# Retention chunk products from one unrounded pass to three rounded passes, in a hybrid decoder kernel on one core

## What is computed

```python
scores = jnp.einsum('bnihd,bnjhd->bnhij', q, k) * intra
inner = jnp.einsum('bnhij,bnjhe->bnihe', scores, v)
k_dec = k * jnp.exp((C - 1 - idx)[:, None] * log_g[None, :])[:, :, None]
kv = jnp.einsum('bnjhd,bnjhe->nbhde', k_dec, v)
...
state * chunk_decay + kv_n, state
...
q_dec = q * jnp.exp((idx + 1.0)[:, None] * log_g[None, :])[:, :, None]
cross = jnp.einsum('bnihd,nbhde->bnihe', q_dec, state_start)
return (inner + cross).reshape(B, S, H, DV)
```

## Time and profile before

| | us |
|---|---|
| median of three runs | 2712.46 |
| the profiled execution | 2713.61 |
| its span on the core | 2711.8 |
| PE busy | 2661.3 |
| VectorE busy | 1643.1 |
| GpSimd busy | 862.8 |
| ScalarE busy | 625.8 |

### The profile page before, as it was taken

One profiled execution on the slowest core, in us unless ns is written; L12 is line 12 of the kernel. 1 busy time (PEld: TensorE's weight loads), 2 busy tenths in 40 slices (PEclk: granted clock), 3 DMA queues, 4 the chain that ended last, 5 costly groups with the idle time before them and its releaser, 6 DMA issues.

```text
span 2711.8 us, 39266 instructions
## 1 busy us (share of the span) xinstructions
PE 2661.3 (98%) x14674; PEld 2260.8 (83%) x14674; DVE 1643.1 (61%) x3712; ACT 625.8 (23%) x1259; POOL 862.8 (32%) x467
## 2 busy tenths in 40 slices
PE   7999999999999999999999999999999999999998
PEld 5888888888888888788878888888888888888886
DVE  6778777877754433534578778777877434453333
ACT  5333333333311111200142332333332111120001
POOL 3333333333321212434542333333332122243443
PEclk9999999999999999999999999999999999999999
DMA  4322222122211112323532222222222111133244
GB/s 169 95 75 63 76 71 82 57 83 64 83 41 39 43 36 71 121 93 118 160 95 83 75 74 65 71 75 78 61 81 62 42 49 41 40 103 100 94 140 140
DMA packets 292832, 217.79 MB, mean 80 GB/s; under 512 B 31682, under 2 KB 246036, under 8 KB 292388
## 3 DMA queue, kind: packets, MB, share of 16 engines
q1 hardware_dynamic: 254322, 151.21, 19.1%
q10 hardware_dynamic: 38322, 64.07, 6.8%
HBM read 176.37 MB, written 38.86 MB: 79 GB/s over the span
## 4 chain that ended last, share of the span: by engine, by line
PE 82%; DVE 7%; DMA 3%; POOL 3%; issue 2%; SPq 1%; ACT 1%; ACTq 0%; DVEq 0%; POOLq 0%
PE dense_ps L739 20%; PE dense_ps L743 20%; PE dense_ps L741 20%; PE work L722 3%; PE dense_ps L763 2%; PE dense_ps L764 2%; PE dense_ps L765 2%; DMA arena<-l_scratch 1%; PE work L975 1%; POOL w_lo L2161 1%; PE work L1012 1%; PE work L951 1%; PE work L934 1%; PE work L1032 1%; PE work L1094 1%
## 5 line engine op out<-in xcount | busy, mean ns | idle before, releaser
L739 PE MATMUL dense_ps<-act_hi,w_hi 128*128 128x512 f32 x2560 | 1065.4, 416 | 11.5 <-POOL act_lo L2182 5.3
L743 PE MATMUL dense_ps<-act_hi,w_lo 128*128 128x512 f32 x2560 | 1003.7, 392 | 0.0
L741 PE MATMUL dense_ps<-act_lo,w_hi 128*128 128x512 f32 x2560 | 1001.5, 391 | 0.0
L2161 POOL TENSOR_TENSOR w_lo<-w_raw,w_hi 128x1024 fp32r<-128x1024 f32 x174 | 435.0, 2500 | 1094.0 <-ACT w_hi L1229 554.1
L743 PEld LDWEIGHTS dense_ps<-act_hi,w_lo 128*128 128x128 f32 x2560 | 481.4, 188 | 106.8
L739 PEld LDWEIGHTS dense_ps<-act_hi,w_hi 128*128 128x128 f32 x2560 | 483.5, 189 | 98.4 <-issue 6.1
L741 PEld LDWEIGHTS dense_ps<-act_lo,w_hi 128*128 128x128 f32 x2560 | 484.2, 189 | 81.2 <-issue 0.2
L1675 DVE SCALAR_TENSOR_TENSOR arena<-arena,cols 128x512 f32<-128x512 f32 x288 | 239.9, 833 | 4.9
L1540 DVE CAST w_hi<-w_raw 128x1024 fp32r<-128x1024 f32 x92 | 67.1, 729 | 173.0 <-PE dense_ps L765 112.7
L722 PE MATMUL work<-mk,arena 128*128 128x128 f32 x768 | 113.8, 278 | 11.4 <-issue 7.5
L1689 DVE SCALAR_TENSOR_TENSOR arena<-arena 128x512 f32<-128x512 f32 x96 | 115.0, 1198 | 15.8 <-ACT arena L1235 15.7
(11 more groups left out here) (216 smaller groups left out, 3792.8 us busy)
## 6 DMA issues: line engine op xcount, KB each, us to landing
w_raw<-in_w_in SPq DMA_DIRECT2D x138, 512.0 KB, 3.7
gate_scratch<-arena ACTq DMA_DIRECT2D x64, 256.0 KB, 2.5
arena<-gate_scratch ACTq DMA_DIRECT2D x64, 256.0 KB, 2.9
arena<-l_scratch SPq DMA_DIRECT2D x62, 256.0 KB
w_raw<-in_w_out SPq DMA_DIRECT2D x18, 512.0 KB, 4.1
o_scratch<-arena ACTq DMA_DIRECT2D x32, 256.0 KB, 2.0
arena<-o_scratch ACTq DMA_DIRECT2D x32, 256.0 KB, 3.3
w_raw<-in_w_up_dn SPq DMA_DIRECT2D x16, 512.0 KB, 4.2
```

The lines of the kernel that those rows point to most:

```text
L739: eng.matmul(dense_ps[:, to, :], w_hi[:, slot, k, :], hi[:, k, seg], start=(k == 0), stop=False)
L741: eng.matmul(dense_ps[:, to, :], w_hi[:, slot, k, :], lo[:, k, seg], start=False, stop=False)
L743: mm = eng.matmul(dense_ps[:, to, :], w_lo[:, slot, k, :], hi[:, k, seg], start=False, stop=(k == KT - 1))
L2161: eng.tensor_tensor(w_lo[:, slot, :, :], w_from[second][:, :, :], w_hi[:, slot, :, :].bitcast(F32), ALU.subtract)\
```

## The change

Each operand of the three chunk products is split in a high part (rounded to float32r, by ACT) and a low part (operand minus high part, by DVE for keys, scores and states, by POOL for values and queries; it takes the operand's place). A product is now three rounded matmuls of 256 columns (`three`). The semaphores rop_f (operand ready), rop_h (high part ready), rop_v and rop_p (low parts ready) count the operands in the written orders. PE waits before a half's first chunk for the low parts of queries, values and scores, and before each queries-times-state product for the state's low part. In the second half 4 filling pieces instead of 2 stand before the chunks and 6 instead of 8 after them. The splits of both z weight blocks no longer wait for the values' block. In the last head, two instead of four delta blocks are rounded by ACT before the first tanh of the second half, the others after the states. Some buffers are placed anew in the arena to make room. The scores' product and the transposes are unchanged.

```diff
--- before
+++ after
+def in_order(*steps):
+    return {step: i + 1 for i, step in enumerate(steps)}
+OPERANDS = in_order("q0", "k0", "s0", "q1", "k1", "s1")
+HIGHS = in_order("v0", "q0", "k0", "s0", "state1", "state2", "state3", "state4", "v1", "q1", "k1", "s1", "state5", "state6", "state7")
+LOWS_VECTOR = in_order("k0", "s0", "state1", "state2", "state3", "state4", "k1", "s1", "state5", "state6", "state7")
+LOWS_POOL = in_order("v0", "q0", "v1", "q1")
...
+        rqd, rqd_lo, rqd_hi = parts("rqd", rt_at, [P, CPH, P])
+        rsc, rsc_lo, rsc_hi = parts("rsc", swap_at, [P, CPH, P])
+        _, rvt_lo = low_parts("rvt_of", rvt_at, [P, NCH, RDV])
...
@@ -671,8 +705,7 @@
                         load_w(m + 4 + j, w_src(l, w_in, RZ0 + j * P + h * RDV))
                     eng.wait_ge(rst_ok.sem, rst_ok.after(t, 0))
-                    eng.wait_ge(rsc_ok.sem, rsc_ok.after(t, 0))
-                    eng.wait_ge(rqd_ok.sem, rqd_ok.after(t, 0))
+                    eng.wait_ge(rop_f.sem, rop_f.after(t, 0))
                     eng.dma_start(rcon, ret[bass.ds(h, 1), :, :].rearrange("h p n -> p (h n)")).then_inc(rc_in.sem, 16)
...
+                    def three(to, a, b, start, stop):
+                        eng.matmul(to, a[0], b[0], start=start, stop=False)
+                        eng.matmul(to, a[0], b[1], start=False, stop=False)
+                        return eng.matmul(to, a[1], b[0], start=False, stop=stop)
...
-                        fill(5 if hf == 0 else 2)
-                        eng.wait_ge(rkd_ok.sem, rkd_ok.after(t, hf + 1))
-                        eng.wait_ge(rv_ok.sem, rv_ok.after(t, 4))
-                        eng.wait_ge(rsc_ok.sem, rsc_ok.after(t, hf + 1))
-                        eng.wait_ge(rqd_ok.sem, rqd_ok.after(t, hf + 1))
+                        fill(5 if hf == 0 else 4)
+                        eng.wait_ge(rop_p.sem, rop_p.after(t, LOWS_POOL[f"q{hf}"]))
+                        eng.wait_ge(rop_p.sem, rop_p.after(t, LOWS_POOL[f"v{hf}"]))
+                        eng.wait_ge(rop_v.sem, rop_v.after(t, LOWS_VECTOR[f"s{hf}"]))
                         for c in range(CPH):
                             cc = CPH * hf + c
                             if cc < NCH - 1:
                                 if c >= 2:
                                     eng.wait_ge(rst_ok.sem, rst_ok.after(t, cc - 1))
-                                eng.matmul(wk[(0, 5)[c % 2]][:, 0:RDV], rkd[:, c, :], rvt[:, cc, :], start=True, stop=True)\
-                                   .then_inc(rkv_ps.sem, 1)
+                                three(wk[(0, 5)[c % 2]][:, 0:RDV], (rkd_hi[:, c, :], rkd_lo[:, c, :]),
+                                      (rvt_hi[:, cc, :], rvt_lo[:, cc, :]), True, True).then_inc(rkv_ps.sem, 1)
                             dst = wk[4 if c < 2 else 1][:, (c % 2) * RDV:(c % 2 + 1) * RDV]
-                            mm = eng.matmul(dst, rsc[:, c, :], rvt[:, cc, :], start=True, stop=(cc == 0))
+                            mm = three(dst, (rsc_hi[:, c, :], rsc_lo[:, c, :]), (rvt_hi[:, cc, :], rvt_lo[:, cc, :]),
+                                       True, cc == 0)
                             if cc:
-                                eng.wait_ge(rst_ok.sem, rst_ok.after(t, cc))
-                                mm = eng.matmul(dst, rqd[:, c, :], rstate[:, cc % 2, :], start=False, stop=True)
+                                eng.wait_ge(rop_v.sem, rop_v.after(t, LOWS_VECTOR[f"state{cc}"]))
+                                mm = three(dst, (rqd_hi[:, c, :], rqd_lo[:, c, :]),
+                                           (rstate_hi[:, cc % 2, :], rstate_lo[:, cc % 2, :]), False, True)
                             mm.then_inc(ro_ps.sem, 1)
-                            fill(1 if c < CPH - 1 else 8)
+                            fill(1 if c < CPH - 1 else 8 if hf == 0 else 6)
                         for _ in fills:
                             pass
...
+                    def z_tanh(hf, e):
+                        eng.wait_ge(dense_ok[e].sem, dense_ok[e].after(m + BLK_RET + 4 + hf, 1))
+                        eng.wait_ge(rsz_ok.sem, rsz_ok.after(t, 2 * hf + e - 1))
+                        eng.activation(rth[:, e, :], dense_ps[:, e, :], ACT.Tanh, scale=0.5).then_inc(rth_ok.sem, 1)
+                    def values_hi(hf):
+                        four = slice(CPH * hf, CPH * hf + CPH)
+                        eng.wait_ge(rv_ok.sem, rv_ok.after(t, 4))
+                        eng.wait_ge(ro_ps.sem, ro_ps.after(t, 0))
+                        eng.activation(rvt_hi[:, four, :], rvt[:, four, :], ACT.Copy).then_inc(rop_h.sem, 1)
+                    values_hi(0)
                     for hf in range(NHALF):
+                        eng.wait_ge(rop_f.sem, rop_f.after(t, OPERANDS[f"q{hf}"]))
+                        eng.activation(rqd_hi[:, :, :], rqd, ACT.Copy).then_inc(rop_h.sem, 1)
+                        eng.wait_ge(rop_f.sem, rop_f.after(t, OPERANDS[f"k{hf}"]))
+                        eng.activation(rkd_hi[:, :, :], rkd, ACT.Copy).then_inc(rop_h.sem, 1)
+                        eng.wait_ge(rop_f.sem, rop_f.after(t, OPERANDS[f"s{hf}"]))
+                        eng.activation(rsc_hi[:, :, :], rsc, ACT.Copy).then_inc(rop_h.sem, 1)
                         if last and hf == 1:
-                            for i in range(KT // 2):
+                            for i in range(2):
                                 o_d_hi(i)
-                        for e in range(2):
-                            eng.wait_ge(dense_ok[e].sem, dense_ok[e].after(m + BLK_RET + 4 + hf, 1))
-                            eng.wait_ge(rsz_ok.sem, rsz_ok.after(t, 2 * hf + e - 1))
-                            eng.activation(rth[:, e, :], dense_ps[:, e, :], ACT.Tanh, scale=0.5).then_inc(rth_ok.sem, 1)
-                            if last and hf == 1 and e == 0:
-                                for i in range(KT // 2, KT):
-                                    o_d_hi(i)
+                        for c in range(CPH):
+                            cc = CPH * hf + c
+                            if cc < NCH - 1:
+                                eng.wait_ge(rst_ok.sem, rst_ok.after(t, cc + 1))
+                                eng.wait_ge(ro_ps.sem, ro_ps.after(t, cc))
+                                eng.activation(rstate_hi[:, (cc + 1) % 2, :], rstate[:, (cc + 1) % 2, :], ACT.Copy)\
+                                   .then_inc(rop_h.sem, 1)
+                            if c == CPH - 2:
+                                z_tanh(hf, 0)
+                        if hf == 0:
+                            values_hi(1)
+                        elif last:
+                            for i in range(2, KT):
+                                o_d_hi(i)
+                        z_tanh(hf, 1)
...
-                    split_w(m + BLK_RET + 5, (BLK_RET + 5) % 2)
+                    eng.wait_ge(dense_ok[1].sem, dense_ok[1].after(m + BLK_RET + 1, 1))
+                    split_w(m + BLK_RET + 5, (BLK_RET + 5) % 2, held=False)
+                    def low(f, hi, lo, of):
+                        eng.wait_ge(rop_h.sem, rop_h.after(t, HIGHS[of]))
+                        eng.tensor_tensor(lo, f, hi.bitcast(F32), ALU.subtract).then_inc(rop_v.sem, 1)
...
                         eng.wait_ge(rpart.sem, rpart.after(t, 4))
                         eng.tensor_tensor(rqd, rkq[:, 1, seg].rearrange("p (c t) -> p c t", c=CPH),
-                                          bcast4(rcon[:, P:2 * P]), ALU.mult).then_inc(rqd_ok.sem, 1)
+                                          bcast4(rcon[:, P:2 * P]), ALU.mult).then_inc(rop_f.sem, 1)
                         eng.wait_ge(rtok_ps.sem, rtok_ps.after(t, hf + 1))
                         eng.tensor_scalar(rkd, chunks(0), rcon[:, 2 * P:2 * P + 1], None, ALU.mult)\
-                           .then_inc(rkd_ok.sem, 1)
+                           .then_inc(rop_f.sem, 1)
                         eng.wait_ge(rsc_ps.sem, rsc_ps.after(t, hf + 1))
-                        eng.tensor_tensor(rsc, chunks(1), bcast4(rcon[:, 0:P]), ALU.mult).then_inc(rsc_ok.sem, 1)
+                        eng.tensor_tensor(rsc, chunks(1), bcast4(rcon[:, 0:P]), ALU.mult).then_inc(rop_f.sem, 1)
+                        low(rkd, rkd_hi[:, :, :], rkd_lo[:, :, :], f"k{hf}")
+                        low(rsc, rsc_hi[:, :, :], rsc_lo[:, :, :], f"s{hf}")
...
+                            if cc < NCH - 1:
+                                new = (cc + 1) % 2
+                                low(rstate[:, new, :], rstate_hi[:, new, :], rstate_lo[:, new, :], f"state{cc + 1}")
...
-                        split_w(m + BLK_RET + 10, (BLK_RET + 10) % 2)
+                        eng.wait_ge(dense_ok[1].sem, dense_ok[1].after(m + BLK_RET + 6, 1))
+                        split_w(m + BLK_RET + 10, (BLK_RET + 10) % 2, held=False)
...
+                    def query_low(hf):
+                        eng.wait_ge(rop_h.sem, rop_h.after(t, HIGHS[f"q{hf}"]))
```

(39 more changed lines are left out.)

## The result

The changed kernel takes **2748.46 us** (median of 4 runs, 2747.25 to 2749.91) against 2712.09 for the kernel before in the same comparison: ratio 1.0132, 95% interval 1.012 to 1.0144. It is slower by 1.3%; 2745 was forecast, in a range of 2721 to 2762. The profiled execution has a span of 2746.9 us, 35.1 over the one before. (The head of the earlier trace rows is the third of the first layer, one of its two middle ones; the line above calls it the second.)

The account below looks back on a forecast made before the run. PE (TensorE), busy 98% of the span, was taken as the bound. Starts 25.8, state's copy 7.7, last heads 5.9, products -10.0 and clock 3.4 sum to +32.8, from 2712.5 to 2745 us; range 2721 to 2762.

Parts of the forecast that it names:

- The products: PE's 176 chunk products: each 0.077 us cheaper, 13.5 us if nothing else moved, 10.0 us counted after absorption.
- rule of four passes: Alternative price of PE's products: three passes save a quarter, 0.109 us each, 19.1 us in all; the forecast sum would be 2741.
- The starts: Before chunk 0 of each head, PE waits for split operands: 3.4, 2.2, 2.2, 5.1 us a layer, 25.8 us in all.
- The state's copy: End of each first half: row statistics some 0.96 us later behind state 4's copy and subtraction, 7.7 us in all.
- The second half: Before the second half's chunks: four pieces last 2.7 us and cover the splitting of operands, so no wait.
- The last head: End of each layer's last head: PE waits 2.9 us more for the next weight's low part, 5.9 us in two layers.
- The clock: PE's granted clock falls once behind each new 5.1 us wait in the last heads: 3.4 us in all.
- at every head's start: Rival: the clock falls at all eight heads' starts, 10.2 us more than forecast, 2755 us; chance 0.17.
- the cover holds: Rival at the heads' starts: rounding and subtractions fit in 3.7 us, the state's second pass hides too, 2699 us; chance 0.07.
- VectorE and POOL don't disturb each other: Rival at the heads' starts: no disturbance in the subtractions, starts cost 18.2 us, sum +25.2, 2738 us; chance 0.18.
- the products are no cheaper: Rival in the chunk products: rounded products cost PE as much as before, +10.0 us, 2755 us; chance 0.03.
- The early splits: Second z weight's split, moved some 10 us ahead into the values stage, has enough cover there; costed at nothing.

Follow-up runs that it names:

- e9: The changed kernel with the edits of e1, e2, e3 and e5, and the six loads, first heads' split, z tanh and silu moved later: 2701.48 us (0.996).
- e1: The changed kernel with the first half's values rounded behind the second value copy, not the fourth, and subtracted before the second z weight's split: 2722.04 us.
- e2: The changed kernel with VectorE's subtraction of state 4 moved behind the row statistics: 2740.08 us (1.0105).
- e7: The changed kernel with two filling pieces instead of four ahead of the second half's chunks, eight instead of six behind: 2760.02 us (1.0177).
- e3: The changed kernel with four delta blocks, not two, rounded early in last heads, the next weight's low part after five blocks, not six: 2744.76 us.
- e5: The changed kernel with the keys' low part made by VectorE from PSUM, one SBUF input instead of two: 2741.91 us (1.0111).
- e10: e9 with a fourth rounded matmul, low part by low part, in each product: 2721.72 us (1.0034).
- e8: The kernel before the change with only the early splits of both z weight blocks added: 2713.37 us (1.0001).
- e6: The changed kernel with the early splits undone, so both z weight blocks' splits wait again for the values' block: 2757.09 us (1.0163).

## Why the prediction was right, step by step

- **The products.** Right: 0.356 us for three rounded passes was read from the values stage, and a chunk of nine passes with one piece lasts 1.77 us (0.684 + 3 x 0.362). 0.077 saved was taken; 0.073 shows in the chunks and 0.081 over a whole head of e9. An unrounded product cost 0.435 us, but a rounded pass 0.115 to 0.1185, more than a quarter of it. The Trainium skill's rule of four passes for true float32 ("FP8 and Floating Point Precision", section "TensorE Precision Notes") would have given 0.109, an estimate; as a price the runs are against it.
- **The starts.** The chain, its order and the turns of VectorE and POOL came as written: waits of 2.9, 1.9, 1.9 and 4.7 us where 3.4, 2.2, 2.2 and 5.1 stood, 23.0 against 25.8 us, and e1 took 17.1 us of them away. Each is 0.3 to 0.5 us short, partly because PE's record of waiting begins when its last matmul ends. In the third head that matmul starts at 983.23 and takes 0.23 us to the next; from there to 985.56 it is 2.1 us, for 2.2 forecast.
- **The state's copy.** Right. 0.91 us for the 0.96 forecast (the prediction's own times, 984.84 and 985.84, are 1.00 apart); the wait before the transposes rose by 1.15 us a head, 9.2 in all, which is these 7.3 and 1.8 of products absorbed there. e2 took 6.1 us of this wait back. No chunk waits for its state.
- **The second half.** Right that four pieces cover it and what the other two are for: with two, 0.87 us are missing (e7), so the four, 1.37 us more, leave 0.5.
- **The last head.** 5.9 us were put down (two times 2.9 are 5.8). The wait for the weight rose from 0.30 to 3.67 us in each of two heads, 6.7 in all, less the products absorbed there (11 x 0.08 in two heads) and 0.8 us from smaller waits next to it: 4 to 5. The mechanism was right; what e3 adds is that it can't be had back there alone.
- **The clock.** The term that was mis-sized: 3.4 us for two falls behind the 5.1 us waits; measured some 9 to 10.5 (35.1 - 38.1 + 13.5 by the sums above, 9.3 by e1, 10.3 at the starts by the granted clock). It fell behind five starts, waits of 1.94 and 2.9 us among them, and cost 1.7 us each there and 2.4 to 2.7 behind the longest waits. The rival "at every head's start" was priced at 13.6, and the truth lies between. That 2745 came within 3.5 us of 2748 is partly luck: the starts' 2.8 us and the last heads' 1 to 2 us too much hid more than half of the clock's 6 to 7 too little.
- **The rivals.** That the cover holds is refuted by the starts themselves. That VectorE and POOL don't disturb each other is refuted by 1.95 against 0.75 us (e5), and that the products are no cheaper by the chunks, e9 and e10.
- **The range.** Its ends add up to 2723 and 2763, given as 2721 and 2762; nothing hangs on it.
- **The early splits** were costed at nothing and cost nothing (e8); what they bring, 8.6 us with the clock's part, shows only with the new work behind them (e6).

## What to carry to other kernels

Splitting operands moves work from an engine that is the bound to three that aren't, and the busy shares say nothing against it; what decides is how long the bound engine works between the moment the last operand exists and the moment it needs the split one. Count that chain instruction by instruction, with the turns that VectorE and GpSimd take at each other, before the products' price. Then start each split as soon as its own part is there, and put copies that nobody needs yet behind the work that somebody waits for: with the same products, these moves, and a low part made from PSUM (e5), were the difference between 2748 and 2701 us.

## What the runs showed of the hardware that was not expected

The same wait of 1.9 us brought PE's clock down to 1.2 GHz at one head and not at the next (0.81 and 0.76 against 1.00). Four heads, two in each layer, have this wait in the traces of the changed kernel, e2, e3 and e7; the clock fell behind one of the four in the first, none in e2, two in e3 and three in e7. So one trace doesn't say what a short wait costs; each fall in the changed kernel's starts cost 1.7 us of work or more, and e1 gained 26.4 us for 17.1 us of waits.

A VectorE instruction with two SBUF inputs that asked while POOL worked went ahead of POOL's next instruction, even where that one was ready: at 981.79 VectorE's keys asked, POOL's queries had been ready since 981.24, and POOL's instruction was 1.72 us long instead of 1.29, with VectorE's turn in it.
